# A two-layer model on one core: a second mixer's preparation laid under the first mixer's levels, and eight weight pieces dealt anew

## The reference, cut to what matters

```python
h = rmsnorm(x, norm_mix[l]);  p = h @ w_in[l]
y_a = hgrn2_mixer(...)            # chunk_gla: S_t = diag(f_t) S_{t-1} + k_t v_t^T
y_b = gated_deltanet_mixer(...)   # chunk_gated_delta: a triangular solve in each chunk of 128 tokens
y_c = rglru_mixer(...)            # a linear recurrence: a = exp(log_a), u = sqrt(1 - a^2) * (i * xc)
y_d = rwkv7_mixer(...)            # a recurrence that here too becomes a triangular solve
x = x + concatenate([y_a, y_b, y_c, y_d]) @ w_out[l]
x = x + memory_cross_attention(rmsnorm(x, norm_xattn[l]), mem_n, wq, wk, wv, wo)   # k = mem_n @ wk, v = mem_n @ wv
...
# in gated_deltanet_mixer and chunk_gated_delta:
q = l2norm(to_heads(q)) * HEAD_DIM ** -0.5;  k = l2norm(to_heads(k))
g = -exp(A_log) * softplus(alpha + dt_bias);  gc = cumsum(g)
rel = exp(where(causal, gc[..., :, None] - gc[..., None, :], -inf))
kb = k * beta;  lower = (kb @ k^T) * rel * strict;  uw = triangular_solve(I + lower, [v * beta, kb * exp(gc)])
scores = (q @ k^T) * rel
```

## Time and profile before

| what | value |
|---|---|
| median of 3 runs | 1986.95 us (1986.77 to 1990.31) |
| profiled execution: its own time | 1990.8 us |
| its span, first to last instruction | 1989.0 us |
| busy: PE, DVE, ACT | 94%, 74%, 57% |
| granted TensorE clock, mean | 0.97 |
| layer 0, input projection to the end of the output projection | about 31 to 308 us |
| layer 1, the same | about 598 to 876 us |
| experts | from about 950 us to the end |
| output projection of layer 0 on PE | ends at 307.9 us; its last chunk takes 5.5 us |
| one chunk of the input projection on PE | 5.76 us |
| the first mixer's output on PE (`outputs_b`) | 1.84 us |
| a load of 1 MB outside the experts, issue to landing | 4.9 to 5.5 us |

### The profile page before, as it was taken

One profiled execution on the slowest core, in us unless ns is written; L12 is line 12 of the kernel. 1 busy time (PEld: TensorE's weight loads), 2 busy tenths in 40 slices (PEclk: granted clock), 3 DMA queues, 4 the chain that ended last, 5 costly groups with the idle time before them and its releaser, 6 DMA issues.

```text
span 1989.0 us, 29716 instructions
## 1 busy us (share of the span) xinstructions
PE 1873.3 (94%) x12520; PEld 1617.3 (81%) x12521; DVE 1466.7 (74%) x1547; ACT 1131.7 (57%) x1065; POOL 0.2 (0%) x4
## 2 busy tenths in 40 slices
PE   7998799999999988899699999999999999999996
PEld 6976688899989877778588888888888888888885
DVE  6767645444457677553698989989899898998985
ACT  5555224443344652143377767777677777777774
POOL 0000000000000000000000000000000000000000
PEclk9998899999999999899799999999999999999998
DMA  7541004255545421023499999999999999999992
GB/s 239 171 149 59 28 23 162 85 191 182 182 145 170 157 78 44 23 92 118 161 345 341 381 345 366 370 330 379 346 369 367 330 380 346 370 365 333 377 374 97
DMA packets 239450, 465.99 MB, mean 234 GB/s; under 512 B 11856, under 2 KB 87760, under 8 KB 239312
## 3 DMA queue, kind: packets, MB, share of 16 engines
q1 hardware_dynamic: 239312, 464.03, 65.6%
HBM read 462.95 MB, written 1.05 MB: 233 GB/s over the span
## 4 chain that ended last, share of the span: by engine, by line
PE 84%; DVE 10%; ACT 3%; issue 2%; DMA 0%; DVEq 0%; SPq 0%; ACTq 0%
PE ps L2077 31%; PE ps L1557 15%; PE ps L2087 15%; PE ps L1542 11%; PE ps L1577 6%; DVE MT L858 4%; PE ps L2133 2%; PE ps L1622 1%; PE ps L2108 1%; ACT MT L438 1%; DVE MT L861 1%; PE ps L2148 1%; DVE MT L864 1%; DVE x L858 1%; DVE TMP L858 1%
## 5 line engine op out<-in xcount | busy, mean ns | idle before, releaser
L1318 DVE TENSOR_TENSOR wlo<-raw,whi 128x2048 fp32r<-128x2048 f32 x140 | 320.4, 2291 | 55.7 <-ACT whi L736 55.5
L736 ACT ACTIVATE whi<-raw 128x2048 fp32r<-128x2048 f32 x140 | 268.9, 1922 | 120.8 <-PE ps L2087 71.2
L871 DVE TENSOR_TENSOR wlo<-raw,whi 128x2048 fp32r<-128x2048 f32 x85 | 194.5, 2289 | 98.9 <-ACT whi L447 98.7
L1318 DVE TENSOR_TENSOR wlo<-PT,whi 128x2048 fp32r<-128x2048 f32 x84 | 192.1, 2292 | 31.2 <-ACT whi L736 30.2
L447 ACT ACTIVATE whi<-raw 128x2048 fp32r<-128x2048 f32 x85 | 162.1, 1907 | 45.2 <-PE ps L1577 43.6
L2077 PE MATMUL ps<-whi,hE_hi 128*128 128x512 f32 x672 | 185.4, 398 | 2.4 <-DVE hE_lo L1387 2.4
L736 ACT ACTIVATE whi<-PT 128x2048 fp32r<-128x2048 f32 x84 | 161.4, 1922 | 34.9 <-PE ps L2077 34.2
L2077 PE MATMUL ps<-wlo,hE_hi 128*128 128x512 f32 x672 | 180.1, 390 | 0.0
L2077 PE MATMUL ps<-whi,hE_lo 128*128 128x512 f32 x672 | 179.8, 389 | 0.0
L2077 PEld LDWEIGHTS ps<-wlo,hE_hi 128*128 128x128 f32 x672 | 126.2, 188 | 27.2
L2077 PEld LDWEIGHTS ps<-whi,hE_lo 128*128 128x128 f32 x672 | 126.1, 188 | 26.7
(11 more groups left out here) (272 smaller groups left out, 3397.5 us busy)
## 6 DMA issues: line engine op xcount, KB each, us to landing
raw<-in_moe_w_up SPq DMA_DIRECT2D x111, 1024.0 KB, 6.8
PT<-in_moe_w_down SPq DMA_DIRECT2D x56, 1024.0 KB, 6.4
PT<-in_moe_w_gate SPq DMA_DIRECT2D x55, 1024.0 KB, 6.7
TMP<-in_moe_w_gate SPq DMA_DIRECT2D x55, 1024.0 KB, 6.6
raw<-in_moe_w_down SPq DMA_DIRECT2D x55, 1024.0 KB, 6.0
raw<-in_w_in SPq DMA_DIRECT2D x28, 1024.0 KB, 5.4
raw<-in_ffn_w_gate SPq DMA_DIRECT2D x11, 1024.0 KB, 5.3
raw<-in_ffn_w_up SPq DMA_DIRECT2D x11, 1024.0 KB, 5.5
```

Of the source, the lines that this page charges most:

```text
L736: nc.scalar.activation(ex_hi[m % XSPL], ex_raw[m % XRAW], ACT.Copy).then_inc(S("w_hi"), 1)
L871: V.tensor_tensor(wlo[i % SPL][:, :], raw[d % RAW][:, :], whi[i % SPL][:, :].bitcast(F32), ALU.subtract).then_inc(S("w_lo"), 1)
L1318: V.tensor_tensor(ex_lo[m % XSPL], ex_raw[m % XRAW], ex_hi[m % XSPL].bitcast(F32), ALU.subtract).then_inc(S("w_lo"), 1)
```

## The change

Four things are changed, in both layers.

1. **Gates and logarithms move into the input projection.** PE does the small products of `gates` ahead of chunk 11 (and in layer 1 the second one ahead of chunk 12). ACT takes their sigmoids and the squares of q and k at chunk 11, and `logs` at chunk 12, now with two table loads that are written out and one more group of logarithms (the norms of q and k). PE sums these squares ahead of chunk 12. The constants of both layers (`lam`, `expa`) are made once, in layer 0. DVE's gates, its `logs`, the running sums and the first two differences stand at chunk 12. The splits of the first three `w_out` chunks no longer stand here but one by one further down. Their buffers lend room (`spare`) to the new operands.
2. **The second mixer's preparation moves into the levels**: `second(v)` on DVE and on PE, and the exponentials, differences and copies on ACT between the levels' own. The first score product of the second mixer follows the last level.
3. **Norm and output of the first mixer, and the end of the third, move into the steps of the second mixer's inverse** (`beside`).
4. **The memory pieces are dealt anew**: four steps ahead of the levels and three in each level (pieces 0 to 2), piece 3 in the last four steps of the first inverse, 4 in its solves, 5 one step at a time in the second inverse, 6 in its solves, and 7 in the attention: four steps before the wait for x and four after the norm. The loads are ordered to match.

Beside these, `tm_add` does one split less before it adds, and the norm that follows does it (in layer 1 after `xattn_wo` there is none to move).

```diff
     for layer in range(DEPTH):
+        w_out = [("tm", "w_out", layer, TM_ROWS * j) for j in range(4)]
+        pieces = [("kv", name, layer, c) for name in ("xattn_wk", "xattn_wv") for c in range(0, D, CM_COLS)]
         out += [("cm", "w_in", layer, c) for c in W_IN_COLS]
-        out += [("tm", "w_out", layer, TM_ROWS * j) for j in range(3)]
-        out += [("kv", "xattn_wk", layer, c) for c in range(0, D, CM_COLS)]
-        out += [("kv", "xattn_wv", layer, c) for c in range(0, D, CM_COLS)]
-        out += [("tm", "w_out", layer, 3 * TM_ROWS)]
+        out += pieces[0:4] + w_out[0:1] + pieces[4:6] + w_out[1:2] + pieces[6:7] + w_out[2:4] + pieces[7:8]
...
-            def cm_evac(n0, count, dst, scale=1.0, after=None):
+            def cm_evac(n0, count, dst, scale=1.0, after=None, upto=None, late=None):
                 for j in range(count):
                     if after:
                         after(j)
                     n = n0 + j
-                    ahead(n + SPL)
+                    ahead(min(n + SPL, upto) if upto else n + SPL)
+                    if late:
+                        late(j)
                     act.wait_ge(S("chunk_done"), n + 1)
                     a(dst(j), ps[:, cm_index[n] % 4, :], ACT.Copy, scale=scale).then_inc(S("cm_free"), 1)
...
+                    logs(l)
+
+            def gates_late(l, j):
+
+                if j != 11:
+                    return
                 act.wait_ge(S("lora_mm"), l + 1)
...
+                a(G_N[0], pt(B_Q), ACT.Square)
+                a(G_N[1], pt(B_K), ACT.Square).then_inc(S("gd_sq"), 1)
 
             def logs(l):
 
-                o, o2 = PCOL["gdn_A_log", l][0], PCOL["lru_lambda", l][0]
                 table("exp_and_others")
...
+                table("natural_log")
...
                 a(col(ST_SP, 8), col(ST_SP, 8), ACT.Ln, bias=1.0).then_inc(S("gd_sp"), 1)
+                act.wait_ge(S("gd_ss"), l + 1)
+                for c in range(2):
+                    a(G_N[c], ps[:, 5 + c, :], ACT.Ln, bias=epsc(0))
                 table("exp_and_others")
+                for c in range(2):
+                    a(G_N[c], G_N[c], ACT.Exp, scale=-0.5).then_inc(S("gd_rn"), 1)
...
             def tm_add(k, n0, count, ahead_to):
 
-                ahead(ahead_to)
+                ahead(ahead_to - 1)
...
+                if j == 12:
...
+                    logs(l)
...
+                def second(v):
+
+                    if v == 0:
+                        dve.wait_ge(S("gd_cum"), 4 * l + 1)
+                        chain.link(lambda: V.tensor_copy(col(ST_GC, 16), ps[:, 6, 0:16]))
+                        tt(col(ST_GD, 8), col(ST_GTOT, 8), col(ST_GC, 8), ALU.subtract).then_inc(S("gd_gd"), 1)
+                        dve.wait_ge(S("gd_rn"), 2 * (l + 1))
+                        stt(pt(B_Q), pt(B_Q), HD ** -0.5, G_N[0], ALU.mult, ALU.mult)
+                    if v == 1:
+                        tt(pt(B_K), pt(B_K), G_N[1], ALU.mult)
+                        dve.wait_ge(S("gd_cum"), 4 * l + 2)
+                        tt(g_kb(l), pt(B_K), ps[:, 5, :], ALU.mult).then_inc(S("gd_ops"), 1)
+                    if v == 2:
+                        dve.wait_ge(S("gd_eg"), l + 1)
+                        tt(g_qe(l), pt(B_Q), tmp(2), ALU.mult)
+                    if v == 3:
+                        dve.wait_ge(S("hg_end"), 2 * (l + 1))
+                        tt(cm(h_kd(l)), cm(tmp(0))[:, :, 0:P], cm(h_kd(l)), ALU.mult).then_inc(S("hg_x"), 1)
+                        tt(h_qe(l), pt(A_Q), h_qe(l), ALU.mult)
+                    if v == 4:
+                        tt(g_kbe(l), g_kb(l), tmp(2), ALU.mult)
+                    if v == 5:
+                        dve.wait_ge(S("gd_rel"), l + 1)
+                        tt(many(g_rel(l), 8), many(g_rel(l), 8), rep(incl, 8), ALU.mult)
+                    if v == 6:
+                        dve.wait_ge(S("state"), 3 * l + 1)
+                        tt(cm(h_state(l)), cm(ps[:, 5, 256:512]), rep(bdones, 2), ALU.mult).then_inc(S("state_bd"), 1)
+
...
+                    take(v - 1)
+                    second(v)
                     rglru(l, v)
...
+                def beside(v):
+
+                    rwkv_ahead(l, v)
+                    if v == 2:
+                        head_out(l, 0, 7, tmp(0), lambda c: pc("hgrn_norm", l, c), pt(A_G), 0)
+                    if v == 4:
+                        rglru(l, LEVELS)
+
+                inverse(2 * l, after=beside)
...
+                ahead(first_chunk["w_out", l] + 1)
...
+                if j == 11:
+                    pe.wait_ge(S("lora_in"), l + 1)
+                    pe.wait_ge(S("lru_ri"), 2 * (l + 1))
+                    for c in range(2):
+                        mm(ps[:, 4, 256 * c:256 * c + 256], sw[0:64, SW_WA + P * c:SW_WA + P * c + P], pt(D_W, 1)[0:64, :])
+                        mm(ps[:, 5, 256 * c:256 * c + 256], sw[64:128, SW_WA + P * c:SW_WA + P * c + P], pt(D_W, 1)[64:128, :])
+                    for c in range(2):
+                        mm(ps[:, 6, 256 * c:256 * c + 256], sw[:, SW_G2 + P * c:SW_G2 + P * c + P], pt(D_G, 1)).then_inc(S("lora_mm"), 1 if c else 0)
+                    if l:
+                        pe.wait_ge(S("sm_ready"), 2 * (l + 1))
+                        for c in range(2):
+                            mm(ps[0:32, 7, 0:256], sw[:, SW_V1 + 32 * c:SW_V1 + 32 * c + 32], pt(D_V + c, 1), start=c == 0, stop=c == 1).then_inc(S("vmix_mm"), 1 if c else 0)
+                if j == 12:
...
+                    pe.wait_ge(S("lora_s"), l + 1)
+                    pe.wait_ge(S("gd_sq"), l + 1)
+                    for c in range(2):
+                        mm(ps[:, 5 + c, :], bdones, G_N[c]).then_inc(S("gd_ss"), 1 if c else 0)
                 if j != 7:
...
+            def second(l, v):
+
+                if v == 0:
+                    pe.wait_ge(S("hg_v"), l + 1)
+                    for c in range(2):
+                        for t in range(TT):
+                            o_ = 256 * c + P * t
+                            w_ = 256 * t + P * c
+                            mm(ps[:, 4, o_:o_ + P], tmp(3)[:, w_:w_ + P], incl)
+                            mm(ps[:, 5, o_:o_ + P], tmp(4)[:, w_:w_ + P], ident).then_inc(S("gd_cum"), 1 if c and t else 0)
+                if v in (2, 3):
+                    p_ = v - 2
+                    if p_:
+                        pe.wait_ge(S("gd_diff"), 2 * l + 1)
+                    else:
+                        pe.wait_ge(S("gd_eg"), l + 1)
+                    for t in range(TT):
+                        for c in range(2):
+                            a_ = at(0, t, c)
+                            k = ST_G + 4 * t + 2 * c + p_
+                            mm(ps[:, 4, a_:a_ + P], col(k).to_broadcast([P, P]), incl).then_inc(S("gd_cum"), 1 if t and c else 0)
+                if v == 4:
+                    pe.wait_ge(S("gd_ops"), l + 1)
+                    pe.wait_ge(S("hg_x"), l + 1)
+                    for c in range(2):
+                        tr(ps[:, 5, P * c:P * c + P], h_kd(l)[:, P * c:P * c + P]).then_inc(S("hg_trk"), 1 if c else 0)
+                if v == 5:
+                    pe.wait_ge(S("hg_kd"), l + 1)
+                    for c in range(2):
+                        mm(ps[:, 5, 256 + P * c:256 + P * c + P], h_kdt(l)[:, P * c:P * c + P], tmp(1)[:, P * c:P * c + P]).then_inc(S("state"), 1 if c else 0)
+
...
+                kv(l, 0, range(KT // 2))
+                pe.wait_ge(S("gd_rn"), 2 * (l + 1))
+                pe.wait_ge(S("gd_wide"), l + 1)
...
+                    for step in range(KT // 2 + 3 * v, min(KT // 2 + 3 * v + 3, 3 * KT)):
+                        kv(l, step // KT, [step % KT])
+                pe.wait_ge(S("gd_ops"), l + 1)
...
+                scores(0, pt(B_K), g_kb(l)).then_inc(S("gd_sc"), 1)
...
+                outputs_b(7, tmp(1), mt(1), h_state(l), h_qe(l)).then_inc(S("o_full"), 1)
+                scores(2, pt(B_K), pt(B_Q)).then_inc(S("gd_sc"), 1)
...
+                    if v >= 3:
+                        pe.wait_ge(S("y_put"), 4 * l + 1)
+                        kv(l, 3, range(2 * v - 6, 2 * v - 4))
...
+                    kv(l, 5, [v, v + 1] if v == LEVELS - 1 else [v])
...
+                kv(l, 6, [0, 1])
...
-                kv(l, 7, [7])
+                kv(l, 6, [6, 7])
...
             def attention(l):
+                kv(l, 7, range(PRE))
                 pe.wait_ge(S("x_done"), 6 * l + 2)
                 norm(2 + 3 * l)
+                kv(l, 7, range(PRE, KT))
```

More of the change, by code:

```diff
@@ L521, in gates_ahead @@
                     if l:
[L522 to L535 removed]
+                        act.wait_ge(S("vmix_mm"), 2)
@@ L890, in stats, with norm @@
                         stt(dst[:, t, :], src[:, t, :], col(t), gain, ALU.mult, ALU.mult).then_inc(S("x_done"), 1)
-            def norm(i, gain, dst):
-                ahead(2)
+            def norm(i, gain, dst, upto):
+                ahead(upto)
                 for c in HI_DVE:
@@ L1015, in logs @@
```

(8 more changed lines are left out.)

535 lines of the change are left out of this document (235 added, 300 removed).

## The result

The changed kernel takes 1966.17 us (median of 4 runs, 1965.08 to 1967.12) where the kernel before, timed beside it, takes 1988.63 (1986.77 to 1990.42): ratio 0.9883, 95% interval 0.9871 to 0.9896, so 1.2% faster. The prediction was 1963.5 in a range of 1950 to 1977. The profiled execution after took 1967.12 us, its span 1965.3; against the one before (span 1989.0) the gain is 23.7 us, forecast 23.2. Executions of the kernel before fall into two groups, here 1986.8 and 1987.0 against 1990.3 and 1990.4, so a gain between two single executions is good to some 4 us, and the profiled one is of the longer group.

A forecast was written before the change was run, and what follows sets the result against it. Chains between gate products and the second mixer's inverse (70.4 and 73.5 us) were taken as the winnable part; layers -10.4 and -9.9 and splits -2.9 make -23.2 us, forecast 1963.5 us, range 1950 to 1977.

The forecast's parts named there:

- The start of the levels: Gate products to first level: 4.9 us in place of 17.7 in layer 0, 6.9 in place of 20.2 in layer 1.
- The preparation under the levels: First level to first inverse, second mixer's preparation included: 42.5 us, with 1.6 of DVE waiting for the small sums.
- (a): First inverse longer by added DVE work and 1.5 us of slow clock: +7.0 us in layer 0, +8.6 in layer 1.
- (b): Solves behind the first inverse: pieces ahead save half of the roughly 2.4 us the slow clock costs, -1.2 a layer.
- (c): Second inverse: each step gets a 0.93 us step of piece 5, of which 0.6 shows; +3.0 us a layer.
- (d): Last solves, where PE is the chain: two more piece steps and four transposes, +2.4 us a layer.
- (e): Attention's norm: four piece steps fill PE's gap and keep its clock, four more stand open; net +1.4 us a layer.
- The splits: Adds into x start 1.5 us earlier: -1.45 us each after `xattn_wo` and layer 0's dense block, nothing at `w_out`.
- a drain at each load: Rival: ACT's three table loads at chunk 12 each hold it as long again; about 1967 us, chance 0.02.
- ACT's backlog: Rival: ACT's lateness at chunks 11 and 12 stalls PE in the projection; 11 us a layer gives about 1985, chance 0.03.
- Cold PE in the first inverse: Rival: its matmuls run at the low clock, +4 us a layer beyond (a), (b) and (e) fail; 1979.5, chance 0.14.
- More is hidden: Rival: level waits and (c) nearly hidden, no cold inverse; -2.5, -2.0 and -1.5 us a layer, 1951, chance 0.15.

The follow-up runs named there:

- `PRE = 0`: The changed kernel with all eight steps of piece 7 behind the attention's norm, none ahead of it: 1976.88 us, ratio 0.9934.
- the fillers of 6: The changed kernel with the third mixer's end behind the first inverse and six useless matmuls in each of three norm gaps: 1962.34 us, ratio 0.9861.

## Why the prediction was right, point by point

**The start of the levels.** Shown. The 17.7 us between the gate products and the first level were for the most part a chain of ACT; it fits under chunks 12 and 13, and putting it back costs 19.4 of the 22.5 us. DVE starts the level 1.4 us behind the projection's end, where I counted 1.35.

**The preparation under the levels.** 42.5 us in layer 0, to the tenth, with the wait for the small sums in it. In layer 1 43.8: the steps of its last level but one ran at the lower clock (4.44 for 2.75). I had the cold in the levels' ends as a rival only; it is there in about half of the layers. I had counted that PE pauses there no longer than in the row of 0.99; the gap of 2.26 us is longer than any in it.

**(a)** The largest miss, +0.6 and +1.7. The base of 40.9 without the clock was never measured by itself; nearest is 41.4, with one cold pair. Against it the inverse is 1.6 and 2.6 us longer, and 2.1 and 3.1 against the base, where I took 1.5; so the mis-sized term is the clock's, within its bounds of 0 to 5. The rival's price of 4 beyond it did not come.

**(b)** The place was right, the size half. Two steps of piece 3 now stand just ahead of the solves, whose first 16 records take 1.28 for 2.15; the number of steps between the solves is the same. So the slow clock's whole price came back, 2.7 and 2.5 us, where I took half of 2.4.

**(c), (d), (e)** (c): 0.54 of each 0.93 within the inverse, for 0.6; that layer 0 shows +3.9 and layer 1 +2.9 is the inverse of the kernel before, 27.7 and 28.7 long. (d): +2.1 for +2.4. (e): right in its mechanism. In layer 0 the norm starts 0.1 later and not 0.5, and the second four steps add 3.3 and not 3.7, so +0.5 for +1.4; in layer 1 the norm of the kernel before took 5.44 and not 6.67, so +1.7. A filled gap keeps the norm near 3.73 us, and that is shown both ways: with `PRE = 0` the same records slow down to 5.44, with filler at other norms they speed up to 3.8. Over all traces the 32 records took 5.1 to 6.7 us behind 32 of 34 open gaps (2.85 to 3.23 us), 3.8 behind the other two, and 3.7 to 3.8 in all 36 cases with the gap filled or under 0.7. The Trainium skill (TensorE: Matmul & The Clock Gate, Part 1) says that idling brings the throttle back; these rows agree, with the two exceptions.

**The splits.** The step that failed. I let the adds start 1.5 us earlier, which they do, but the second pair waits for PE's last half and then takes 1.41, whatever is done before: 0.3 us a site. The -1.8 at each `xattn_wo` holds 0.3 of this in layer 0 and none in layer 1, where the gap was 2.94 already; the most of it, 1.2, is the clock, the norm at 5.44 in place of 6.67. At the two `w_out` ends, which I gave nothing, it is 0.8 each, for another reason: a split that stands first waits there for a load. That the gaps of all five sites add up to 2.2, near my 2.9, is chance.

**The total.** That the gain of 23.7 us came within 1 us is in part luck. The start of the first inverse and (a) cost 1.4 and 2.3 more than forecast over both layers; (b) gave 2.8 more, and the two norms behind `xattn_wo` 2.4 that no term holds: in that execution of the kernel before they took 6.67 and 6.66, a length that the same code takes in some variants of the changed kernel as well (6.68 to 6.74).

Of the rivals, *a drain at each load* and *ACT's backlog* did not happen: no product of the projection waits for ACT. *Cold PE in the first inverse* is there, but not at its price, and (b) and (e) did not fail with it. *More is hidden* and *the levels go cold* are out for the whole; the latter is true of one level in about half of the layers.

## What to carry to other kernels

Look for the engine that has a long chain on one side of a phase and idles on the other: moved under the products it held nothing up, though three table loads were in it. When two engines take turns, count both sums step by step after each move: the bound changes sides within one loop, and small pieces of independent work belong where the other engine's gap is, not dealt evenly; that dealing was most of the last 7 us here. A last add that waits for the last half of a product is hardly helped by an earlier start of the first half (0.3 us of 1.45 here); what helps is to keep a wait for a load out of its way (0.8).

## What the runs showed of the hardware that was not expected

Unchanged code in unchanged order comes out at one of two lengths, by where TensorE's granted clock stands between its two levels (1.2 and 2.4 GHz). Over ten executions with the levels' code unchanged, level 0's mask step to the inverse took 40.6 to 40.9 us in five and 42.2 to 42.3 in the other five, in layer 0. The norm behind `xattn_wo` took 3.8, 5.1, 5.4 or 6.7 us for the same 32 records behind the same gap of 2.9. And the experts' part took 1029.4 to 1029.7 us in some executions and 1032.1 to 1032.5 in others; PE at its start in a run of the second kind (with the fillers of 6):

```profile
949.50 6.12 PE L2210 MATMUL ps<-MT,PT 128*128 128x128 f32 x32
958.01 2.08 PE L2154 MATMUL ps<-whi,hE_hi 128*128 128x512 f32 x4 [2.39 <-DVE hE_lo L1448]
959.88 1.76 PE L2154 MATMUL ps<-wlo,hE_hi 128*128 128x512 f32 x4
```

and in the changed kernel:

```profile
955.67 5.12 PE L2204 MATMUL ps<-MT,PT 128*128 128x128 f32 x32
963.18 1.21 PE L2148 MATMUL ps<-whi,hE_hi 128*128 128x512 f32 x4 [2.40 <-DVE hE_lo L1449]
```

The clock comes back at another record of the same sequence. So an edit upstream can move 2 to 3 us in a stretch that it doesn't touch, and a difference of that size between two kernels says nothing of the edit until the stretches are compared one by one. What decides at which record it comes back stays open.
